# A state-space layer in chunks of four tokens, with the chunk matrices built in the feed-forward layer ahead of it

## What is computed

```python
def s5_layer(h, w_in, a_re, a_im, log_dt, b_re, b_im, c_re, c_im, d, w_glu):
    u = h @ w_in                                  # 256 x 1024: 64 groups of 16 channels
    lam_bar = jnp.exp(lam * dt)                   # complex, 64 states for each group
    b_bar = ((lam_bar - 1.0) / lam)[..., None] * b_mat
    bu = jnp.einsum('gpc,bsgc->bsgp', b_bar, u_g)
    ...                                           # states: s_t = lam_bar * s_(t-1) + bu_t
    y = jnp.einsum('gcp,bsgp->bsgc', c_mat, states).real.reshape(B, S, D_MODEL)
    g = jax.nn.gelu(y + d * u)
    val, gate = jnp.split(g @ w_glu, 2, axis=-1)
    return val * jax.nn.sigmoid(gate)
```

## Time and profile before

| | us |
|---|---|
| median of 3 runs | 2737.49 (2734.57 to 2745.36) |
| profiled execution, own time | 2734.69 |
| its span (first to last instruction) | 2733.0 |
| PE busy in the span | 2280.9 (83%) |
| DVE busy | 1724.9 (63%) |
| ACT busy | 1079.3 (39%) |
| POOL busy | 735.9 (27%) |
| feed-forward layer 0, slices 1 to 21 | 1480.0 to 1653.4 |
| s5in projection and what surrounds it | 1653.4 to 1682.6 |
| scan stage, to the first glu matmul | 1682.6 to 1895.8 |

### The profile page before, as it was taken

One profiled execution on the slowest core, in us unless ns is written; L12 is line 12 of the kernel. 1 busy time (PEld: TensorE's weight loads), 2 busy tenths in 40 slices (PEclk: granted clock), 3 DMA queues, 4 the chain that ended last, 5 costly groups with the idle time before them and its releaser, 6 DMA issues.

```text
span 2733.0 us, 40794 instructions
## 1 busy us (share of the span) xinstructions
PE 2280.9 (83%) x15156; PEld 1926.7 (70%) x15160; DVE 1724.9 (63%) x2631; ACT 1079.3 (39%) x1527; POOL 735.9 (27%) x522
## 2 busy tenths in 40 slices
PE   5998768688678865875999997667999699999997
PEld 2864545677466555764969996224999599887997
DVE  3488463477458545765557667997666766654665
ACT  3221533376432534664444333001433333445432
POOL 2320032488452135883240000783000000000000
PEclk7995889899788888997999998777999899999999
DMA  5248702499526125995415452000545244442442
GB/s 232 93 185 323 246 0 107 185 341 343 209 77 234 44 88 205 323 321 185 160 42 202 174 208 77 0 0 31 185 184 200 100 162 184 164 152 72 175 184 92
DMA packets 93046, 443.72 MB, mean 162 GB/s; under 512 B 9088, under 2 KB 25600, under 8 KB 56704
## 3 DMA queue, kind: packets, MB, share of 16 engines
q1 hardware_dynamic: 79104, 390.10, 39.1%
q0 software_dynamic: 8496, 31.99, 3.0%
q10 hardware_dynamic: 5328, 20.04, 1.8%
HBM read 401.20 MB, written 40.89 MB: 162 GB/s over the span
## 4 chain that ended last, share of the span: by engine, by line
PE 39%; DVE 6%; POOLq 2%; POOL 2%; ACT 2%; DVEq 2%; issue 1%; DMA 0%; ACTq 0%
PE bank L645 12%; PE bank L644 11%; PE bank L646 11%; DVE ring_halves L380 2%; POOLq L593 1%; ACT high L1248 1%; POOLq L598 1%; PE bank L1098 1%; POOL XT L591 1%; PE bank L1075 1%; PE bank L1088 1%; DVEq L2301 1%; PE bank L1161 1%; POOL XT L594 1%; PE bank L686 1%
## 5 line engine op out<-in xcount | busy, mean ns | idle before, releaser
L644 PE MATMUL bank<-ssdb_halves,high 128*128 128x256 f32 (+1 forms) x2080 | 613.2, 295 | 62.3 <-DVE HT_halves L1683 34.9
L645 PE MATMUL bank<-HT_halves,high 128*128 128x256 f32 (+1 forms) x2096 | 623.7, 298 | 0.0
L646 PE MATMUL bank<-ssdb_halves,ring_halves 128*128 128x256 f32 (+1 forms) x2080 | 612.3, 294 | 0.0
L380 DVE TENSOR_TENSOR ring_halves<-ring,high 128x2048 fp32r<-128x2048 f32 (+1 forms) x200 | 414.8, 2075 | 157.7 <-ACT high L1248 157.5
L1248 ACT CAST high<-ring 128x2048 fp32r<-128x2048 f32 x230 | 437.2, 1903 | 134.1 <-PE bank L646 134.1
L380 POOL TENSOR_TENSOR ring_halves<-ring,high 128x1024 fp32r<-128x1024 f32 (+1 forms) x96 | 363.6, 3789 | 375.3 <-ACT high L1248 375.3
L644 PEld LDWEIGHTS bank<-ssdb_halves,high 128*128 128x128 f32 x2080 | 398.3, 192 | 81.9 <-issue 55.1
L645 PEld LDWEIGHTS bank<-HT_halves,high 128*128 128x128 f32 x2096 | 398.9, 190 | 9.1
L646 PEld LDWEIGHTS bank<-ssdb_halves,ring_halves 128*128 128x128 f32 x2080 | 394.6, 190 | 9.7
L389 DVE TENSOR_TENSOR dring_halves<-dring,dhigh 128x1024 fp32r<-128x1024 f32 (+1 forms) x152 | 226.0, 1487 | 154.7 <-ACT dhigh L1254 148.5
L1254 ACT CAST dhigh<-dring 128x1024 fp32r<-128x1024 f32 x152 | 160.5, 1056 | 238.2 <-PE bank L646 238.1
(11 more groups left out here) (426 smaller groups left out, 4384.1 us busy)
## 6 DMA issues: line engine op xcount, KB each, us to landing
ring<-in_ffn SPq DMA_DIRECT2D x88, 1024.0 KB, 5.4
ring<-in_moe SPq DMA_DIRECT2D x64, 1024.0 KB, 7.5
ring<-in_ada SPq DMA_DIRECT2D x48, 1024.0 KB, 7.0
dring<-in_ffn_down SPq DMA_DIRECT2D x88, 512.0 KB, 3.5
dring<-in_moe_down SPq DMA_DIRECT2D x64, 512.0 KB, 4.6
ring<-in_foxin SPq DMA_DIRECT2D x24, 1024.0 KB, 4.8
ring<-in_win SPq DMA_DIRECT2D x22, 1024.0 KB, 4.8
zs_b<-x_slots POOLq DMA_DIRECT2D x32, 512.0 KB, 8.6
```

The costliest lines, as they stand in the source:

```text
L380: eng.tensor_tensor(low, w, h, ALU.subtract).then_inc(sem(f"low_{engine}"), 1)
L644: mm(o, a[0], b[0], start=first, stop=last and bool(kw), **kw)
L645: mm(o, a[0], b[1], start=False, stop=last and bool(kw), **kw)
L646: return mm(o, a[1], b[0], start=False, stop=last, **kw)
```

## The change

**Chunks.** The 256 tokens are taken as 64 chunks of four. For each lot of 128 states the scan now runs over 64 chunk states, and four lots fit side by side in one DVE instruction of 256 columns, so there are 8 turns (c = 0 to 7) in place of 32, with the same DVE instructions. `fade` holds |lam|^4 with zeros where a lot begins, so that one scan instruction treats four lots.

**Matrices.** The inputs of a chunk state are a product of the four tokens' channels (4 x 32 = 128 rows) with lam^(3-s) * b_bar. The output of each token is a product of the chunk state before it with C * lam^(s+1), plus the direct effect of the tokens of its own chunk, a lower triangular block matrix K with d on its diagonal. So for each lot there are 128x128 matrices: two for inputs, one K, two for outputs. They depend on the parameters alone.

**Building.** They are built in the 22 slices of layer 0's feed-forward layer, which is now written out slice by slice on PE, ACT and DVE. In each of slices 1 to 16 DVE does one complex product (`times`: two instructions of 512 elements and two of 256), in place of `s5_matrices`. In slices 5 to 8 and 13 to 16 ACT spreads powers of B into blocks and PE turns them (8 transposes); in 9 to 12 and 17 to 20 ACT spreads powers of C and PE forms K (8 matmuls with 128 columns, 4 with 32). ACT copies both from PSUM one slice later. POOL writes the results to DRAM (`s5_bc`, `s5_kr`) and makes the cos and sin tables for 64 chunks (`s5_turns`: six steps on twice the states, one call before the slices with blocks and one between bT and the output blocks). The rotations of before, in the attention layer and beside the scan, are gone.

**The S5 layer.** SP loads the matrices back as eight tiles of 1 MB and eight of 512 KB (`tables`). The tokens of a chunk must come onto different partitions: `move` does that with 16 DMAs for each half of u, and 16 for each half of the result on the way back; the last 16 (`s5_last_move`) stand behind three glu tiles. Each turn has 8 input matmuls and 20 output matmuls with 64 (or 63) columns on 128x128 weights. `s5_dmat` and `s5_turn` are gone. The first two glu groups are interleaved over the channels.

The core of the diff:

```diff
+            def s5_moves(t0):
+
+                def tables(c):
+                    if c < RING:
+                        sp.wait_ge(sem("down_free"), DOWN_AT["ffn", 0] + FFN_SLICES)
+                    else:
+                        sp.wait_ge(*at("s5_pe", ("out", c - RING)))
+                    sp.dma_start(dring[c % RING][:], s5_kr[c]).then_inc(*done(f"s5_kr{c % RING}", c, 16))
+                    load(t0 + c, s5_bc[c])
+
+                def move(half, dst, src, key):
+                    for s_ in range(STEP):
+                        for q in range(BATCH):
+                            sp.dma_start(dst(s_, q, half), src(s_, q, half)).then_inc(*done(f"moved{half}", key, 16))
...
+                for n in ("s5_bt_kept", "s5_c_kept", "s5_k_kept0", "s5_k_kept1", "s5_loaded"):
+                    sp.wait_ge(*at(n, "last"))
+                for c in range(2):
+                    tables(c)
+                sp.wait_ge(*at("s5_dve", ("u_sb", 3)))
+                move(0, to_rel, from_nat, "u")
+                for c in range(2, RING):
+                    tables(c)
+                sp.wait_ge(*at("s5_dve", ("u_sb", KC - 1)))
+                move(1, to_rel, from_nat, "u")
+                for c in range(RING, KC):
+                    tables(c)
+                sp.wait_ge(*at("s5_act", ("y", 3)))
+                move(0, to_nat, from_rel, "y")
...
+            def s5_turns(half):
...
+                own = slice(S5_HALF * half, S5_HALF * half + S5_HALF)
+                for n in range(6):
                     d = 1 << n
-                    low, new = tab[:, :, :, 0:d], tab[:, :, :, d:2 * d]
-                    cos, sin = (pw[:, n, i, bass.ds(BATCH * batch, BATCH)].unsqueeze(1).unsqueeze(3)
-                                .to_broadcast([P, 2, BATCH, d]) for i in range(2))
-                    tmp = table_tmp[:, :, :, 0:d]
+                    low, new, tmp = rot[:, :, :, 0:d], rot[:, :, :, d:2 * d], rot_tmp[:, :, :, 0:d]
+                    cos, sin = (pw[:, n + 2, i, own].unsqueeze(1).unsqueeze(3).to_broadcast([P, 2, S5_HALF, d]) for i in range(2))
                     ptt(new, low, cos, ALU.mult)
...
+                for c in range(BATCH):
+                    pool.dma_start(s5_kr[BATCH * half + c][:, BATCH * P:D].rearrange("p (a t) -> p a t", a=2),
+                                   rot[:, :, BATCH * c:BATCH * c + BATCH, :].rearrange("p a b t -> p a (b t)"))\
+                        .then_inc(*done("s5_loaded", "rot" if half == 0 else "last", 16))
...
+            def s5_keep_out(c):
+                pool.wait_ge(*at("s5_act", ("e_blk", c)))
+                for i in range(2):
+                    pool.dma_start(s5_bc[c][:, (2 + i) * BATCH * P:(3 + i) * BATCH * P].rearrange("p (b c) -> p b c", b=BATCH),
+                                   e_blk[:, i, :, 1:, :].rearrange("p b s c -> p b (s c)"))\
+                        .then_inc(*done("s5_c_kept", c if c < KC - 1 else "last", 16))
+
...
+            def s5_keep_k(c):
+                pool.wait_ge(*at("s5_act", ("k", c)))
+                for s_ in range(STEP):
+                    rows = slice(QUAD * s_, QUAD * s_ + QUAD)
+                    pool.dma_start(s5_kr[c][rows, 0:BATCH * P].rearrange("p (a b) -> p a b", a=BATCH)[:, :, QUAD * s_:P],
+                                   k_blk[c % 2][0:QUAD, :, 0:P - QUAD * s_])\
+                        .then_inc(*done(f"s5_k_kept{c % 2}", c if c < KC - 2 else "last", 16))
...
+                    if half == 0:
+                        pool.wait_ge(*at("s5_loaded", "rot"))
+                        s5_turns(1)
+                    for c in range(BATCH * half, BATCH * half + BATCH):
+                        s5_keep_out(c)
+                        if c > BATCH * half:
+                            s5_keep_k(c - 1)
+                    s5_keep_k(BATCH * half + BATCH - 1)
+                pool.wait_ge(*at("s5_loaded", "last"))
+                m2 = s5p[:, 1, :].unsqueeze(2).to_broadcast([P, S5_CH, CHUNKS - 1])
...
+            def s5_build(j):
+
+                half, c = j // 13, (j - 5) % 4 + 4 * (j // 13)
+                if 5 <= j <= 8 or 13 <= j <= 16:
+                    pe.wait_ge(*at("s5_act", ("x_blk", c)))
+                    for q in range(BATCH):
+                        for i in range(2):
+                            mm_ = nc.tensor.transpose(ps[6 + q // 2][:, (2 * (q % 2) + i) * P:(2 * (q % 2) + i + 1) * P],
+                                                      x_blk[:, i, q].rearrange("p s c -> p (s c)"), ident)
+                    mm_.then_inc(*done("s5_pe", ("turned", c)))
...
+                if 9 <= j <= 12 or 17 <= j <= 20:
+                    pe.wait_ge(*at("s5_act", ("e_blk", c)))
+                    pe.wait_ge(*at("s5_dve", ("e", c // 4)))
+                    for q in range(BATCH):
+                        o = ps[6 + c % 2][0:QUAD, q * P:q * P + P]
+                        for i in range(2):
+                            mm(o, b_one[:, i, (BATCH * c + q) % S5_HALF, :], e_blk[:, i, q, 0:STEP, :], start=q == 0 and i == 0,
+                               stop=False, skip_group_check=True)
+                        mm_ = mm(o[:, 0:QUAD], ident[:, 0:QUAD], skip_diag[:, (BATCH * c + q) % S5_HALF, :], start=False, stop=True,
+                                 skip_group_check=True)
+                    mm_.then_inc(*done("s5_pe", ("k_sums", c)))
...
+                if build is not None:
+                    for j in range(slices):
+                        build(j)
+                        if j + 2 < slices:
+                            gate_up(j + 2, 0)
+                        down(j, 0)
+                    return
...
+                def inputs(c):
...
+                    pe.wait_ge(*at(f"moved{c // BATCH}", "u"))
+                    w = ring[t % RING][:, 0:2 * BATCH * P].rearrange("p (b a s) -> p b a s", b=BATCH, a=2)
                     for i in range(2):
...
+                        for q in range(BATCH):
+                            mm_ = mm(ps[c % 2][:, i * T + q * CHUNKS:i * T + q * CHUNKS + CHUNKS], w[:, q, i, :], u_rel[:, q, c, :],
+                                     start=True, stop=True)
+                    mm_.then_inc(*done("s5_pe", ("in", c)))
...
+                def outputs(c):
...
+                    y = ps[2 + c % 2]
+                    for q in range(BATCH):
+                        mm(y[:, q * CHUNKS:q * CHUNKS + CHUNKS], dring[c % RING][:, q * P:q * P + P], u_rel[:, q, c, :],
+                           start=q == 0, stop=False, skip_group_check=True)
+                    pe.wait_ge(*at("s5_dve", ("states_done", c)))
+                    for q in range(BATCH):
+                        for part in range(2):
+                            for n in range(2):
+                                z = s5_q[:, c % 2, n, part, q * CHUNKS:q * CHUNKS + CHUNKS - 1]
+                                mm_ = mm(y[:, q * CHUNKS + 1:q * CHUNKS + CHUNKS], w[:, part, q, :], z,
+                                         start=False, stop=part == 1 and n == 1, skip_group_check=True)
+                    mm_.then_inc(*done("s5_pe", ("out", c)))
+                    pe.drain().then_inc(sem("tile_free"), 1)
...
+                def turned(c):
+                    act.wait_ge(*at("s5_pe", ("turned", c)))
+                    if c:
+                        act.wait_ge(*at("s5_bt_kept", c - 1))
+                    for i in range(2):
+                        copied = nc.scalar.copy(b_turned[:, 2 * i:2 * i + 2], ps[6 + i][:].rearrange("p (b a s) -> p b a s", b=2, a=2))
+                    copied.then_inc(*done("s5_act", ("bt", c)))
...
+                def blocks(c):
...
+                    q = BATCH * (c % BATCH)
+                    for g in range(2):
+                        rows = slice(64 * g, 64 * g + 64)
+                        nc.scalar.copy(x_blk[rows, :, :, :, 16 * g:16 * g + 16].rearrange("p a b s c -> p a (b s) c"),
+                                       x_pow[rows, :, q:q + BATCH].rearrange("p a b s c -> p a (b s) c"))
+                        copied = nc.scalar.copy(b_one[rows, :, q:q + BATCH, 16 * g:16 * g + 16], x_pow[rows, :, q:q + BATCH, STEP - 1, :])
+                    copied.then_inc(*done("s5_act", ("x_blk", c)))
...
+                if 6 <= j <= 9 or 14 <= j <= 17:
+                    turned((j - 6) % 4 + 4 * (j // 14))
+                if 10 <= j <= 13 or 18 <= j <= 21:
+                    sums((j - 10) % 4 + 4 * (j // 18))
+                if 5 <= j <= 8 or 13 <= j <= 16:
+                    blocks((j - 5) % 4 + 4 * (j // 13))
+                if 9 <= j <= 12 or 17 <= j <= 20:
+                    out_blocks((j - 9) % 4 + 4 * (j // 17))
...
+            def s5_build(j):
...
+                def times(x, re, im, out, conj):
+                    f_re, f_im = (pv(i)[:, own].unsqueeze(1).unsqueeze(3).to_broadcast([P, 2, S5_HALF, 16]) for i in (re, im))
+                    a, b = s5_tmp
+                    tt(a, x, f_re, ALU.mult)
+                    tt(b, x, f_im, ALU.mult)
```

(34 more changed lines are left out.)

372 lines of the change are left out of this document (210 added, 162 removed).

## The result

The changed kernel takes 2775.97 us (median of 4 runs, 2773.93 to 2777.79) where the kernel before takes 2738.53 (4 runs, 2734.57 to 2745.36): a ratio of 1.0137, 95% interval 1.0117 to 1.0157. It is 37 us slower; the forecast was +32 us and 2768.

What follows compares the result with a forecast made beforehand. PE was taken to bound the kernel nearly everywhere, DVE the scan stage. The feed-forward layer's +138 us (83 + 32 + 15 + 5 + 3) less 106 in the scan stage gave +32, about 2768 us, range 2745 to 2795.

Steps and rivals of the forecast that it cites:

- The chain PE, ACT, PE, +83: Layer 0 feed-forward, slices 5 to 20: PE waits uncovered for ACT's copies, then does its building work; +83 us.
- The clock of the slices, +32: Slices 5 to 20: PE's idle gaps drop its clock, costing 2 us a slice; +32 us, ends 0 and 50.
- rival 3: Gaps in the slices leave the clock at full and POOL is in time: -15 us, 2722; chance 0.10.
- POOL's rotations in slice 10, +15: ACT waits for POOL's second half of rotations and DMAs before overwriting e_blk; +15 us once, ends 0 and 22.
- Slices 1 to 3, +5: POOL's first half of rotations falls in slices 1 to 3, where DVE sets the pace; +5 us.
- The last K, +3: Layer's end: ACT's first x_high waits until POOL has written out the last K; +3 us, ends 0 and 8.
- Scan stage at half clock, 96.5 us, tail 12: PE bounds the turns at 12.3 us, stage 96.5 us; last exchange on SP adds 12; net -106 us.
- Which clock?: Scan stage: half clock taken, from the first turn's 2.5 us hole among short streams; -106 us, against -147 at full.
- rival 1: PE's f32 products in the scan stage keep full clock: 138 - 147 = -9 us, 2728; chance 0.22.
- Rival 5, the four passes alone: Four passes alone set f32 matmul cost, so DVE bounds scan turns at 5.3 us: -18 us, 2720; chance 0.03.
- Rival 2, the copies covered: ACT's copies in the slices finish before down(j-1) ends, so PE adds only its own 26 us: 2680; chance 0.05.
- Rival 4, slow exchanges: 64 small DMAs on SP take 15 us more per group, three times on the path: 2813; chance 0.08.

Runs made afterwards that it cites:

- run 1: Changed kernel with PE taking the building of slice j behind gate_up(j+2) instead of ahead of it: 2698.62 us.
- run 7: Changed kernel plus 15 bf16 matmuls of 512 columns on zeros where PE waits in each of slices 5 to 20: 2742.55 us.
- run 2: Changed kernel with both sets of POOL's rotations made in the attention layer ahead: 2750.29 us.
- run 3: Changed kernel with DVE adding the two turned-back state terms, so PE does 8 output matmuls a turn instead of 16: 2749.01 us.
- run 4: Changed kernel with twelve bf16 matmuls of 512 columns on zeros filling PE's wait in the scan stage's first turn: 2734.88 us.
- runs 4 and 5: Run 5 is run 4 with its twelve fillers replaced by true f32 matmuls of 64 columns: 2735.48 us.
- run 9: Changed kernel with the changes of run 1, run 2 and run 4 together, and the single output product of run 3 added: 2635.37 us.
- run 10: Run 9 plus three bf16 matmuls of 512 columns ahead of each later wait for the states in the scan stage: 2625.5 us.

## Why the prediction was right, point by point

- *The chain PE, ACT, PE, +83.* Shown by run 1, and sized by run 7: 82. PE's waits were 3.5 us a slice, as the sum had them for the sums of K (1.1 + 0.5 + 1.7 + 0.1 = 3.4). When they are hidden, a slice with transposes is 1.4 us longer than the 8.5 before on average and one with sums 2.7. PE's own work was put at 0.9 and 2.4; what the rest is, no run tells.
- *A row under another name.* The 30 matmuls in 3.40 us that gave a transpose 0.11 us are L884 and L885, products of rounded halves with the identity, with one record each; they are not the transposes that the change adds. The price holds all the same: in slice 5 the new transposes start 0.11 us apart.
- *The clock of the slices, +32.* Shown by run 7: 30. With it *rival 3* falls, which had the clock at full in the slices.
- *POOL's rotations in slice 10, +15.* Right in kind (run 2), a little small: ACT waited 18.2 us, and the slice was 17 us longer than its neighbours. POOL stood still for 5.7 us ahead of the rotations, with no wait that the trace names; the sum had nothing for it. *Slices 1 to 3, +5*: 6.6 measured, and gone with the rotations.
- *The last K, +3.* Not seen: ACT's first x_high at the layer's end starts at 1792.13, 0.5 us behind the DVE instruction that it needs, and the trace shows no wait for POOL's writes.
- *Scan stage at half clock, 96.5 us, tail 12.* The turns were 12.44 us, the tail about 12.6, since the issues were 0.63 us apart. The pair of weight load and short matmul costs 0.213 us at half clock (run 3) and 3.74 / 32 = 0.117 at full (run 4). The columns that stream do not set it: with 16 a pair takes 0.22 us at half clock. That it is the weight load is inferred. By the Trainium skill (TensorE: Matmul & The Clock Gate, LDWEIGHTS (loading the stationary operand)) a load takes its own columns divided by 1.2 in ns, for 128 columns an estimate of 107 ns, and the trace is near it at full clock (117 ns), not at half (213).
- *Which clock?* The level was right, and that was partly luck. I had put it on the hole together with the short streams, and runs 4 and 5 show that without the hole the stream keeps 1.00. But the row that I rested it on, L871 at 0.50 throughout, had a gap of 4.20 us ahead of it, so it said nothing of a gap of 2.5, and 2.67 had left 1.00. The half clock cost 41 us, what the prediction's two sums differ by (147 - 106). So rival 1 was one gap of 2.44 us away.
- *Rival 5, the four passes alone.* It falls: even at full clock the turn is 6.70 us, not 5.3. By the Trainium skill (FP8 and Floating Point Precision, TensorE Precision Notes) a true f32 matmul is four passes; for 64 columns at 2.4 GHz that makes an estimate of 0.107 us a matmul, 0.053 a pair, and the runs show 0.117 a pair.
- *Rival 2, the copies covered.* It was not so in this kernel; run 1 makes it so by one line and lands at 2699. Its 2680 had 15 us for slice 10; there the wait grew to 22.8 us on ACT, with PE's clock at half for 23.9 us.
- *Rival 4, slow exchanges.* No engine waits for a move inside the stage; only the last exchange is exposed.
- *Not foreseen*: 2 us in s5in. PE's gap in its dense stretch is 3.04 us, where it was 2.67, and behind it 18 matmuls start in 3.4 us at half clock where some 29 fit at full. u is also written in another order, 0.61 us an instruction where it was 0.42.
- *A slip in the last step*: +32 on the median of 2737.5 is 2769.5, not 2768.

```profile
1809.22 0.35 PE L757 MATMUL bank<-ssdb_halves,high 128*128 128x256 f32 x1 [3.04 <-DVE ring_halves L401]
```

```profile
1810.60:1814.00 3.40, 3.40 (x18) 3.40 (x17) 2.10 (x2) 0.00 (x0) 0.00 (x0) 0.50 0.14 37
```

## What to carry to other kernels

When work is hung into a loop on an engine without slack, look at where in the turn it stands: behind the engine's own next long block, the copies it needs are free; ahead of it, PE, ACT and PE run one after the other, 16 times here. After shortening an engine's work, look at the granted clock of the stage, not only at its busy time: a hole of 2.44 us cost 41 us, and twelve matmuls on zeros in it gave them back. A true f32 matmul with 64 columns cost no less than one with 16, so count matmuls there, not columns.

## What the runs showed of the hardware

- The same stream of f32 matmuls with 63 and 64 columns, two products a turn, ran 56 us at 1.00 in run 4 and 95.6 us at 0.50 in the changed kernel, with the same gaps of 0.26 us between turns. The stage kept whichever level it had; what differed was one idle stretch at its start. All six traces that have this stretch unfilled (2.43 to 3.20 us) fell to 0.50 around it and stayed there for 68 to 96 us.
- In dense streams with 256 columns the clock came back: there the half clock behind a gap of 2 to 3 us lasted 3.4 us (s5in above). And the length of such a gap does not decide alone whether it falls. In the attention layer's first product all fourteen kernels have the same code and the same gap of 2.54 us; eight traces have 0.50 behind it, and six keep 1.00. A gap of 2.73 us ahead of slice 5's transposes left 1.00 in the changed kernel and not in run 2. What decides stays open. The rows are the kernel before, then the changed one:

```profile
1323.04 0.36 PE L644 MATMUL bank<-high,ssdb_halves 128*128 128x256 f32 x1 [2.54 <-DVE ring_halves L380]
1320.99 0.36 PE L757 MATMUL bank<-high,ssdb_halves 128*128 128x256 f32 x1 [2.54 <-DVE ring_halves L401]
```

```profile
1323.00:1326.40 3.40, 3.36 (x28) 3.25 (x28) 2.10 (x1) 0.26 (x1) 0.00 (x0) 1.00 0.32 133
1322.50:1325.90 3.40, 3.40 (x18) 3.18 (x16) 0.55 (x1) 0.37 (x1) 0.00 (x0) 0.50 0.00 0
```

- Among the short streams the clock fell behind gaps of less than 1 us (run 9), and not where gaps of 0.26 us alone were left (the later turns of runs 4 and 10). Whether the short streams make a gap count more, or what the engine did before it, no run here tells apart.
- Filling matmuls on zeros cost little where the engine waited anyway: in run 10 they raised PE's work and lowered the time by 10 us; in run 7 two of the sixteen slices got longer by 0.3 and 1.7 us.
